# One-core mixer layer: pooling weights multiplied into the projection weights once, and low parts of weights kept in DRAM

## The reference, cut to what matters

```
h    = layer_norm(x) * (1 + scale) + shift          # shift, scale, gate from silu(c) @ w_ada
xa, ga, u, v, gb = split(h @ w_in)                  # five blocks of 512 columns
pooled_g = window_mean_w(xa_g) - xa_g               # causal mean over tokens, w = 2, 4, 8, 16 for g = 0..3
ya_g = (pooled_g @ w_pool_g) * pool_scale * silu(ga_g)      # w_pool_g is 128 x 128
yb_g = gelu(u_g) * (tril(w_sgu_g) @ layer_norm(gelu(v_g)) + b) * silu(gb_g)
out  = layer_norm(2**0.25 * x + gate * (concat(ya, yb) @ w_out)) * ln_g + ln_b
```

## Time and profile before

| | us |
|---|---|
| median of three runs | 678.67 |
| the profiled execution, its own time | 678.93 |
| span in its profile | 677.2 |
| PE busy | 664.5 |
| DVE busy | 525.6 |
| ACT busy | 239.3 |
| bytes moved by DMA | 106.68 MB |

### The profile page before, as it was taken

The page is one execution under the profiler, slowest core; times in us unless marked ns, Lnnn a source line. Parts: engine busy times, 40 slices in busy tenths (PEclk is TensorE's granted clock), DMA queues, the critical chain, the costliest instruction groups (busy, mean ns, idle before and its releaser), DMA issues.

```text
span 677.2 us, 8864 instructions
## 1 busy us (share of the span) xinstructions
PE 664.5 (98%) x3087; PEld 552.9 (82%) x3087; DVE 525.6 (78%) x973; ACT 239.3 (35%) x316; POOL 61.9 (9%) x77
## 2 busy tenths in 40 slices
PE   8999999999999999999999999999999999999995
PEld 7888787878888888888888888888888888888884
DVE  5879989859769868759969967776978977555876
ACT  4444434338213333326511333334721333323300
POOL 2000200100012101100002201000002210000010
PEclk9999999999999999999999999999999999999998
DMA  8993352883425442575324362288233463224011
GB/s 332 396 370 131 125 187 88 169 300 129 142 76 186 168 176 93 97 210 223 126 94 155 124 248 93 93 109 324 93 124 123 136 245 117 95 81 162 38 63 62
DMA packets 33976, 106.68 MB, mean 158 GB/s; under 512 B 6509, under 2 KB 7569, under 8 KB 33938
## 3 DMA queue, kind: packets, MB, share of 16 engines
q1 hardware_dynamic: 33938, 106.22, 47.6%
HBM read 97.80 MB, written 8.40 MB: 157 GB/s over the span
## 4 chain that ended last, share of the span: by engine, by line
PE 89%; DVE 5%; issue 3%; ACT 1%; DMA 1%; POOL 0%; SPq 0%; POOLq 0%; DVEq 0%; ACTq 0%
PE bank_b L1008 59%; PE bank_a L1008 26%; PE bank_a L1122 2%; DVE gate_rows L723 1%; DMA x_norm<-in_x 1%; PE bank_b L1068 1%; DVE x_stats L622 1%; PE bank_b L1032 0%; ACT h_high L476 0%; ACT w_high L466 0%; DVE w_low L601 0%; DVE y_low L829 0%; PE bank_b L1087 0%; PE bank_b L1059 0%; DVE mixed L818 0%
## 5 line engine op out<-in xcount | busy, mean ns | idle before, releaser
L1008 PE MATMUL bank_b<-h_high,w_high 128*128 128x512 f32 x512 | 202.1, 395 | 0.6 <-DVE sgu_bias L757 0.6
L1008 PE MATMUL bank_b<-h_low,w_high 128*128 128x512 f32 x512 | 199.4, 390 | 0.0
L1008 PE MATMUL bank_b<-h_high,w_low 128*128 128x512 f32 x512 | 199.4, 389 | 0.0
L466 ACT ACTIVATE w_high<-w_float 128x1024 fp32r<-128x1024 f32 x100 | 105.5, 1056 | 149.5 <-DMA w_float<-in_w_units 56.3
L601 DVE TENSOR_TENSOR w_low<-w_float,w_high 128x1024 fp32r<-128x1024 f32 x100 | 122.1, 1221 | 42.5 <-ACT w_high L466 42.3
L1008 PEld LDWEIGHTS bank_b<-h_high,w_high 128*128 128x128 f32 x512 | 96.2, 188 | 21.0 <-issue 1.8
L1008 PEld LDWEIGHTS bank_b<-h_high,w_low 128*128 128x128 f32 x512 | 96.1, 188 | 20.2
L1008 PEld LDWEIGHTS bank_b<-h_low,w_high 128*128 128x128 f32 x512 | 96.2, 188 | 19.7 <-issue 0.5
L411 POOL TENSOR_TENSOR z_rstd<-z_var_eps,minus_half 128x1 f32<-128x1 f32 x16 | 22.0, 1377 | 367.3 <-DVE z_var_eps L858 357.4
L1008 PE MATMUL bank_a<-w_high,y_high 128*128 128x512 f32 x128 | 49.8, 389 | 0.0
L1008 PE MATMUL bank_a<-w_low,y_high 128*128 128x512 f32 x128 | 49.8, 389 | 0.0
(11 more groups left out here) (180 smaller groups left out, 945.4 us busy)
## 6 DMA issues: line engine op xcount, KB each, us to landing
w_float<-in_w_units SPq DMA_DIRECT2D x104, 512.0 KB, 3.3
x_norm<-in_x SPq DMA_DIRECT2D x16, 512.0 KB, 4.4
z<-in_x SPq DMA_DIRECT2D x16, 512.0 KB, 5.5
out<-z SPq DMA_DIRECT2D x15, 512.0 KB, 4.7
z<-in_mod_units SPq DMA_DIRECT2D x12, 512.0 KB, 9.6
x_norm<-in_x_channels SPq DMA_DIRECT2D x12, 512.0 KB, 13.8
mod_spare<-in_mod_units SPq DMA_DIRECT2D x6, 512.0 KB, 8.2
x_norm<-in_w_units SPq DMA_DIRECT2D x4, 512.0 KB, 4.3
```

Source lines behind the costliest of these rows:

```text
L466: nc.scalar.activation(wH[:, n % S_SLOTS, :], wF[:, n % F_SLOTS, :], ACT.Copy).then_inc(w_high, 1)
L1008: last = mm(bank, wl if n == 2 else wh, ml if n == 1 else mh, start=start and n == 0, stop=stop and n == 2)
```

## The change

1. **w_pool goes into the xa weights.** `fold_xa(g)` on PE multiplies, for each of the eight blocks of 128 input channels, the xa unit of group g (now stored turned, so that it can be the stationary operand) by `w_pool_g`: eight float32 matmuls of 128 columns. `fold_copy(g)` on ACT copies the result over the unit's float tile, from where it is split like any unit, and `store_xa(g)` stores it to DRAM (`xa_units`), where the later chunks load it from. The four folds stand in chunk 0: g = 0 among the early products, g = 1 after unit 6, g = 2 after unit 8, g = 3 after unit 10. Units 12 and 16 of chunk 0 land in two spare tiles (`XA_ALONE`).
2. **The pool products go**, in all four chunks, with the splitting of the pooled values on ACT and DVE and of `w_pool`. `y_pool` now reads the pooled values directly, and stands one step after `pooling`.
3. **Low parts of the weights are stored in chunk 0 and loaded after.** `store_low(n)` stores `wL` of all 28 units to `low_units`; in chunks 1 to 3 `load_low` loads the low part of unit n + 2 in step n, and DVE makes no low parts there (but for the last units of chunk 3). `load_w` then waits for the high part of the unit that held the slot, not for the low part.
4. Small moves: `gate_bias` on DVE goes from the early part to step 15, `w_pool` is loaded earlier, DVE does `h_split(0, 1)` ahead of `early_low(4)`.

```diff
 # SP
 def load_w(c, n):
-    wait(sp, w_low, c * UNITS + n - F_SLOTS + 1)
-    sp.dma_start(wF[:, n % F_SLOTS, :], w_units[n % UNITS]).then_inc(w_landed[n % F_SLOTS], 16)
+    held = n - F_SLOTS
+    if isinstance(c, int) and c * UNITS + held < UNITS:
+        wait(sp, w_low, held + 1)
...
+    else:
+        sp.wait_ge(w_high, c * UNITS + held + 1)
...
+    if first and n == XA_UNITS[1] + F_SLOTS:
+        sp.wait_ge(xa_stored, 32)
...
+def store_xa(g):
+    sp.wait_ge(fold_copied, g + 1)
+    sp.dma_start(xa_units[g], xa_float(g)).then_inc(xa_stored, 16)
+def store_low(n):
+    sp.wait_ge(w_low, max(n + 1, len(EARLY)))
...
+    sp.dma_start(low_units[n], w_of(0, n)[1].bitcast(F32)).then_inc(stored, 16)
+def load_low(c, n):
...
+    sp.wait_ge(unit_done, c * UNITS + n - S_SLOTS + 1)
+    sp.dma_start(wL[:, n % S_SLOTS, :].bitcast(F32), low_units[n % UNITS]).then_inc(low_landed[n % S_SLOTS], 16)
...
+            store_xa(0)
+            sp.wait_ge(xa_stored, 16)
             load_early(2)
...
                 for n in range(V_UNITS if first else 0, UNITS):
+                    if first and n == V_UNITS + 2:
+                        sp.wait_ge(gate_added, GATE_UNITS)
+                        for i, unit in enumerate(XA_ALONE):
+                            sp.dma_start(w_float(c, unit), w_units[unit]).then_inc(xa_landed[i], 16)
+                        store_xa(1)
                     if n + 2 * AHEAD < IN_UNITS + 4 or not last:
                         load_w(c, n + 2 * AHEAD)
+                    if first and V_UNITS < n < FIRST_LOOP:
+                        for unit in ((4, 5, 6, 7), (0, 1), (2, 3))[n - V_UNITS - 1]:
+                            store_low(unit)
+                    if first and FIRST_LOOP <= n + AHEAD < UNITS:
+                        store_low(n + AHEAD)
+                    if (first and n + AHEAD >= UNITS) or (not first and not last) or (last and n + AHEAD < IN_UNITS):
+                        load_low(c, n + AHEAD)
 # ACT
+def fold_copy(g):
+    act.wait_ge(folded, g + 1)
+    for half, bank in enumerate(fold_banks(g)):
+        done = nc.scalar.activation(xa_float(g)[:, half * T:(half + 1) * T], bank, ACT.Copy)
+    done.then_inc(fold_copied, 1)
...
             h_evacuate(0, 0)
+            h_evacuate(0, 1)
+            fold_copy(0)
             early_high(4)
-            h_evacuate(0, 1)
 # DVE
             def y_pool(c, g):
-                dve.wait_ge(pool_done, c * G + g + 1)
+                dve.wait_ge(pooled, c * G + g + 1)
...
             def y_low(c, g, high, low, row, src):
                 dve.wait_ge(high, c * G + g + 1)
+                if isinstance(c, int) and c == 0 and g == 0:
+                    dve.wait_ge(v_low_stored, V_UNITS * 16)
...
-                    if not (last and n in LAST_SPLITS_IN):
+                    if first and n + AHEAD < UNITS:
                         split_low(c, n + AHEAD)
 # PE
-            def pool_product(c, g):
...
+            def fold_xa(g):
...
+                for k in range(KT):
+                    cut = slice(k * P, (k + 1) * P)
+                    last = mm(banks[k // 4][:, k % 4 * P:(k % 4 + 1) * P], xa_float(g)[:, cut],
+                              wpF[:, g * P:(g + 1) * P], start=True, stop=True)
...
-                    pe.wait_ge(w_low, c * UNITS + n + 1)
+                    if first:
+                        pe.wait_ge(w_low, n + 1)
+                    else:
+                        pe.wait_ge(w_high, c * UNITS + n + 1)
+                        pe.wait_ge(low_landed[n % S_SLOTS], ((c - 1) * (UNITS // S_SLOTS) + n // S_SLOTS + 1) * 16)
```

More of the change, by code:

```diff
@@ L54 @@
 FIRST_LOOP = 8
+XA_UNITS = tuple(V_UNITS + 4 * g for g in range(G))
+FOLD_AFTER = {6: 1, 8: 2, 10: 3}
+XA_ALONE = (12, 16)
+GATE_BIAS_IN = 15
 LAST_SPLITS_IN = {18: (20,), 19: (21, 22), 20: (23, 24, 25, 26, 27)}
@@ L180, in hybrid_layer @@
         unit_done = sem("unit_done")
+        low_stored = [sem(f"w_low_stored{i}") for i in range(S_SLOTS)]
+        v_low_stored = sem("v_w_low_stored")
+        low_landed = [sem(f"w_low_landed{i}") for i in range(S_SLOTS)]
         vec_turned, vec_ready = sem("vec_turned"), sem("vec_ready")
@@ L188, in hybrid_layer @@
         e_done, e_ready = sem("e_done"), sem("e_ready")
-        small_high, small_low = sem("small_high"), sem("small_low")
+        bias_halved = sem("sgu_bias_halved")
+        folded, fold_copied = sem("xa_folded"), sem("xa_folded_copied")
+        xa_landed = [sem(f"xa_landed{i}") for i in range(len(XA_ALONE))]
+        xa_stored, pool_landed = sem("xa_stored"), sem("w_pool_landed")
         gate_summed, gate_ready = sem("gate_summed"), sem("gate_ready")
@@ L251, in early_float, with landed_at, w_float, xa_float @@
             return (wF[:, 0, :], wF[:, 1, :], gateB[:, :], wS[:, :])[EARLY_LANDING[unit]]
+        def landed_at(c, n):
+            early = sum(1 for u in EARLY if EARLY_LANDING[u] == n % F_SLOTS) - len(EARLY) // F_SLOTS
+            first = isinstance(c, int) and c == 0
+            early -= sum(1 for u in XA_ALONE if u % F_SLOTS == n % F_SLOTS and not (first and n < u))
+            return (c * (UNITS // F_SLOTS) + n // F_SLOTS + 1 + early) * 16
+        def w_float(c, n):
+            if isinstance(c, int) and c == 0 and n in XA_ALONE:
+                return mS[:, XA_ALONE.index(n), :]
+            return wF[:, n % F_SLOTS, :]
+        def xa_float(g):
+            return w_float(0, XA_UNITS[g])
+        def fold_banks(g):
+            return (B[:, 0, :], B[:, 1, :]) if g == 0 else (A[:, 0, :], A[:, 1, :])
         def mod_column(k):
@@ L463, in split_high @@
                 wait(act, unit_done, c * UNITS + n - S_SLOTS + 1)
-                before = sum(1 for u in EARLY if EARLY_LANDING[u] == n % F_SLOTS) - len(EARLY) // F_SLOTS
-                act.wait_ge(w_landed[n % F_SLOTS], (c * (UNITS // F_SLOTS) + n // F_SLOTS + 1 + before) * 16)
-                nc.scalar.activation(wH[:, n % S_SLOTS, :], wF[:, n % F_SLOTS, :], ACT.Copy).then_inc(w_high, 1)
+                if isinstance(c, int) and c == 0 and n in XA_ALONE:
+                    act.wait_ge(fold_copied, XA_UNITS.index(n) + 1)
+                else:
+                    act.wait_ge(w_landed[n % F_SLOTS], landed_at(c, n))
+                nc.scalar.activation(wH[:, n % S_SLOTS, :], w_float(c, n), ACT.Copy).then_inc(w_high, 1)
             def h_evacuate(c, k):
@@ L520, in _ @@
             nc.scalar.activation(X[:, HALO:], B[:, 0, :], ACT.Copy).then_inc(xa_copied, 1)
+            fold_copy(1)
             split_high(0, FIRST_LOOP)
@@ L539, in chunk @@
                             nc.scalar.activation(gv[:, j, :], A[:, j, :], ACT.Gelu).then_inc(v_gelu, 1)
+                    if first and n - 1 in FOLD_AFTER:
+                        fold_copy(FOLD_AFTER[n - 1])
                     g, step = (n - V_UNITS - 1) // 4, (n - V_UNITS - 1) % 4
@@ L548, in chunk @@
                             wait(act, gb_gated, c * G + g)
+                            if g == 0 and not first:
+                                act.wait_ge(z_stats, c * TILES)
                             nc.scalar.activation(tanh[:, :], B[:, 1, :], ACT.Tanh, scale=0.5).then_inc(ga_tanh, 1)
-                            act.wait_ge(pooled, c * G + g + 1)
-                            nc.scalar.activation(pH[:, :], S[(g + 1) % 2][:, HALO:], ACT.Copy).then_inc(p_high, 1)
                         if step == 2:
@@ L882, in first_branches @@
                 v_norm_of(c, 3)
+                y_low(c, 0, yp_high, yp_low, 0, yP)
             def chunk(c, first, last):
@@ L913, in chunk @@
                         if step == 1:
-                            pooled_low(c, g)
-                            wait(dve, yp_ready, c * G + g)
                             gate(ga_tanh, ga_gated, sga, 1, c * G + g + 1)
+                            y_pool(c, g)
                         if step == 3:
-                            if first and g == 0:
-                                dve.wait_ge(small_low, 1)
                             wait(dve, ys_ready, c * G + g)
@@ L936, in chunk @@
                             y_low(c, g, ys_high, ys_low, G + g, mixed)
+                    if first and n == GATE_BIAS_IN:
+                        gate_bias()
                     if last and n in LAST_SPLITS_IN:
```

122 lines of the change are left out of this document (68 added, 54 removed).

## The result

The changed kernel was slower: 691.99 us (691.44 to 692.75, four executions) against 678.86 us, ratio 1.0197, 95% interval 1.0179 to 1.0215. The forecast was 679.1 us, the range ended at 684.0. Two further sets of executions, on two different chips, gave 686.32 us (682.75 to 687.78, ratio 1.0106, 1.0066 to 1.0145) and 683.98 us (682.03 to 686.52, ratio 1.0089, 1.0068 to 1.0110): slower each time, and by differing amounts.

A forecast was written before the change was run, and what follows sets the result against it. PE, busy 664.5 of 677.2 us, was taken as the bound. 678.93 - 11.2 (pool products) + 7.1 (folds) - 1.8 (old waits) + 0.5 + 0.9 + 5.0 (new waits) gave 679.4 us, median 679.1; range 674.0 to 684.0.

The forecast's parts named there:

- any new wait of PE is paid in full: On PE, whose own waits were 2.2 us in all: each new wait adds its own length, clock full throughout.
- Unit 19: Chunks 1 and 2: low part late behind the token stores; PE waits 2.9 and 2.1 us, +5.0, bounds 0 and 5 per chunk.
- Unit 10: Chunk 0: split waits on DVE behind `y_low`, which waits for the stored v parts; +0.9 us, bounds 0 and 4.
- A long receipt for writes: Chunk 0 stores: by a Trainium skill rule, the wait would be some 2 us longer, and the sum 2 us higher.
- Unit 20 of chunk 0: Float of unit 21 lands late, gate copies on ACT behind it; 1 us of room, so 0, bound 2.
- The early fold: Chunk 0, ACT: `fold_copy(0)` ahead of unit 4's split makes its low part late; +0.5 us, bounds 0 and 2.1.
- the fold arithmetic: PE: 16 pool products removed, -11.2 us; four folds of eight float32 matmuls added in chunk 0, +7.1; old waits, -1.8.
- The sum without low parts: Profiled execution: 678.93 - 11.2 + 7.1 - 1.8 = 673.0 us, then +0.5 for the early fold.
- DVE's relief: Chunks 1 to 3: some 80 instructions of 1.22 us leave DVE; PE was not waiting for them, so 0.
- The low parts land in time: Rival: 4-byte stores pass in 9 us instead of 11, nothing waits in step 19; 674.1 us, chance 0.27.
- The queue stays full past unit 20: Rival, step 18 of chunks 1 and 2: 512 KB takes over 1.37 us, unit 20 late too; 684.1 us, chance 0.2.
- The stores of chunk 0 are late: Rival: each store waits 2 us for its receipt, adding 3 to 4 us at unit 10; 682.6 us, chance 0.12.

The follow-up runs named there:

- the second profile: Profile of the changed kernel run again, unedited, on a second chip beside the kernel before; that set measured 686.32 us, ratio 1.0106.
- the folds alone: The changed kernel without stored or loaded low parts, DVE making them in every chunk again: 673.55 us, ratio 0.9923 to the kernel before.
- the best pair: mod_sum(5) put ahead of early_low(4), on the folds alone (672.35 us) and on the changed kernel with x, z loads moved and v stores in one step (672.31 us).

## Why the prediction was wrong, point by point

The profiled execution missed by 692.45 - 679.4 = 13.1 us. The terms below add to 13.1.

- **The step that failed: "any new wait of PE is paid in full", with the clock counted as full throughout.** A wait is paid more than in full. Behind the gaps at units 10, 19 and 19 the units took 7.35, 8.29 and 7.33 us instead of 5.46: +6.6 us, half of the miss, and none of my rivals had it. Of this, 5.8 us are the lower clock. The rest comes with any gap: in the second profile unit 10 stood behind 1.73 us at full clock and took 5.73.
- **Unit 19: right mechanism and place, mis-sized.** "PE waits 2.9 us in chunk 1 and 2.1 in chunk 2" became 5.3 and 3.2: +3.5. Two parts were off. The low part landed 23.5 and 21.4 us after the token store, where I had 20.1 and 19.3 from unit 21's landings before; in the second profile it was 21.7 and 20.0. What grew is the stretch under the 4-byte stores: in chunk 1 the last of the four x loads landed 20.9 us after the token store, 18.3 before, and the two transfers behind it 1.3 us apart, as counted. And PE was ready 18.3 us after the token store in both profiles, not 17.2: the token store did not move as late against PE as I had it. In the second profile the errors nearly cancel, 3.5 + 1.8 = 5.3 against my 5.0.
- **Unit 10.** The path was right, the v stores, then `y_low`, then the split. The wait was 2.0, not 0.9: +1.1. Unit 10's load landed 4.2 us after its issue instead of 3.3, and the seven transfers behind it 1.45 us apart instead of 1.28, so the last v store was there at 91.0, not 89.3; PE came 0.6 late too. A long receipt for writes did not show: `store_xa(1)`, alone in the queue, landed 2.6 us after its issue, where the loads of this size have a median of 3.3.
- **Unit 20 of chunk 0.** I had found 1 us of room and taken 0, bound 2. PE waited 1.3: +1.3. ACT's split of unit 21 waited 11.1 us for its DMA, and the gate copies stood behind it until 157.7, when PE started. The respread x and z loads of chunk 0 took this wait away too, as its cause in that queue would have it.
- **The early fold: costed right.** Chunk 0 was 2.9 us later after the early units, where fold 0 and its queue were to cost 2.3: +0.6. But 0.5 of it stood there before the fold. The 36 small matmuls at the start of the kernel took 7.1 us in this execution, 6.1 before and 6.4 in the folds alone, and the first product of the v units started at 17.69 instead of 17.15. From there the early units took 2.35 us longer than before, in the folds alone 2.3.
- **Right: the fold arithmetic.** The sum without low parts is 673.0 + 0.5 for the execution; the folds alone measured 673.55, their profiled execution 673.27. The first fold took 1.80 us in the chain, the second 1.80. Chunk 3 was 2.9 us shorter (2.8 predicted). DVE's relief was worth 0, as the best pair shows.
- **The rivals.** "The low parts land in time" came true only by moving loads: 673.64 against its 674.1. "The queue stays full past unit 20" named 684.1, and the third set has 683.98, but that is luck: its condition, 512 KB in over 1.37 us, was not met, the saturated windows moving 409 to 412 GB/s, 1.28 us, and PE did not wait for unit 20 in chunks 1 and 2. The figure of about 358 GB/s, which the Trainium skill (DMA: Bandwidth & Descriptors, Bandwidth) has bind transfers between HBM and a core, and of which it says that it is a core's share when both cores of a pair stream, did not bind here, where the kernel ran on one core. "The stores of chunk 0 are late" by 3 to 4 us: no, 1.1 over the forecast.

## What to carry to other kernels

Price a new wait of TensorE with the clock behind it: a gap of 2 to 5 us cost up to 2.9 us more, and not in each execution, so a kernel with gaps also becomes one with a spread. When a change adds transfers, the sum of bytes matters less than what stands in the queue behind a store of many tiny elements: here 54 MB more were free once the loads without hurry, x and z, stood behind the urgent ones and the v stores were issued in one step. And test the halves of a double change alone; here one half gained 5 us and the other lost up to 18.

## What the runs showed of the hardware

- **Gaps and the clock.** Over the ten profiles with gaps of TensorE above 0.8 us (after 80 us; nine of them with stored low parts, and the kernel before), fourteen gaps of 0.9 to 1.81 us were followed by no drop of the granted clock; of five of 1.83 to 2.08 us, four were (1.83, 1.91, 2.02, 2.07, not 2.08); all five from 3.2 to 5.3 us were. A gap filled with matmuls was not. This is no sharp bound: the two groups of executions with gaps near 1.75 us (675.2 and 677.1 us on average, with the x and z loads moved) suggest a drop in some of them. The unit behind a drop took 7.3 to 8.4 us, behind a gap without one 5.7 to 5.8, so the lower clock cost 1.6 to 2.7 us each time.
- **4-byte stores stop the other transfers, not their own queue alone**: 0 to 68 GB/s for twelve us, with the DMA engines all but idle in the first two us of them (share 0.01).
- **A wait can carry a name that only coincides.** All three profiles of the changed kernel name ACT's split, which ended 0.29 us before PE started, since two neighbouring transfers land one spacing apart. Swapping the two told them apart.
